# Experts stage of an encoder layer: the order of two products on the tensor engine, and three operations moved between engines

## The reference, cut to what matters

```
u = peer_u[idx]
a = gelu(einsum('td,ted->te', xb, u))
w = g * a
out = einsum('te,ted->td', w, peer_v[idx])
```

## Time and profile before

| | us |
|---|---|
| median of 3 runs | 4590.63 (4588.02 to 4590.66) |
| the profiled execution | 4585.41 |
| its span, first to last instruction | 4583.5 |
| PE busy in the span | 3587.8 (78%) |
| DVE busy | 3410.8 (74%) |
| ACT busy | 1299.2 (28%) |
| POOL busy | 943.7 (21%) |

### The profile page before, as it was taken

One profiled execution on the slowest core, in us unless ns is written; L12 is line 12 of the kernel. 1 busy time (PEld: TensorE's weight loads), 2 busy tenths in 40 slices (PEclk: granted clock), 3 DMA queues, 4 the chain that ended last, 5 costly groups with the idle time before them and its releaser, 6 DMA issues. The chain is left out here.

```text
span 4583.5 us, 62754 instructions
## 1 busy us (share of the span) xinstructions
PE 3587.8 (78%) x19538; PEld 1972.0 (43%) x19538; DVE 3410.8 (74%) x7568; ACT 1299.2 (28%) x2576; POOL 943.7 (21%) x1038
## 2 busy tenths in 40 slices
PE   7946567997899255333379999999999999999994
PEld 3525443553455122333334445444445445444442
DVE  1034341222679778999969999999999999999998
ACT  2132132211233223222223323323323323333321
POOL 0000000000000000000024444444444444444344
PEclk9966578998999677555589999999999999999997
DMA  2200012101110100333378888888888888888885
GB/s 87 82 3 0 0 80 101 42 14 60 65 38 31 58 0 15 97 111 111 99 271 329 337 320 324 337 328 329 328 330 330 335 318 331 338 326 335 323 323 192
DMA packets 238989, 856.89 MB, mean 187 GB/s; under 512 B 16080, under 2 KB 119312, under 8 KB 167440
## 3 DMA queue, kind: packets, MB, share of 16 engines
q0 software_dynamic: 73728, 536.90, 31.0%
q1 hardware_dynamic: 165136, 318.63, 20.0%
HBM read 792.55 MB, written 62.91 MB: 187 GB/s over the span
## 5 line engine op out<-in xcount | busy, mean ns | idle before, releaser
L1563 POOL COPY x_index<-expert 128x1 uint32 (+1 forms) x512 | 340.6, 665 | 3194.0 <-POOLq L1370 2316.4
L69 PE MATMUL x_ps_v<-x_v_hi,x_w_hi 128*128 128x512 f16 x1536 | 604.5, 394 | 137.2 <-DVE x_w_lo L1667 70.5
L1566 POOL DMA_INDIRECT x_rows<-in_peer_uv,x_index x512 | 579.6, 1132 | 406.9 <-POOL x_index L1563 393.1
L1637 DVE SCALAR_TENSOR_TENSOR acc<-x_rows,x_share,acc 128x1024 f32<-128x1024 f32 x512 | 655.0, 1279 | 0.0
L1721 PE MATMUL x_ps_a<-h_hi,x_u_hi 128*128 128x256 f16 (+1 forms) x2048 | 620.1, 327 | 15.4 <-ACT x_u_hi L1579 14.7
L1722 PE MATMUL x_ps_a<-h_lo,x_u_hi 128*128 128x256 f16 (+1 forms) x2048 | 619.8, 326 | 0.0
L70 PE MATMUL x_ps_v<-x_v_lo,x_w_hi 128*128 128x512 f16 x1536 | 603.7, 393 | 0.0
L71 PE MATMUL x_ps_v<-x_v_hi,x_w_lo 128*128 128x512 f16 x1536 | 602.8, 392 | 0.0
L1590 ACT ACTIVATE x_dots<-x_dots 128x1 f32<-128x1 f32 x512 | 103.9, 203 | 1335.1 <-DVE x_dots L1655 1335.1
L1446 PE MATMUL g_ps<-g_hot_g,g_hot_j 128*128 128x128 f16 x768 | 170.9, 310 | 325.7 <-DVE g_hot_g L1430 325.7
L1655 DVE CUSTOM_DVE_ANT_0 x_rows<-h_lo,x_rows 128x1024 f32<-128x1024 f32 x256 | 312.4, 1220 | 126.5 <-DMA x_rows<-in_peer_uv,x_index 125.3
(11 more groups left out here) (284 smaller groups left out, 6834.7 us busy)
## 6 DMA issues: line engine op xcount, KB each, us to landing
x_u_st<-in_peer_u_t SPq DMA_DIRECT2D x128, 512.0 KB, 6.1
x_v_st<-in_peer_v SPq DMA_DIRECT2D x128, 512.0 KB, 6.3
gate_scratch<-g_out SPq DMA_DIRECT2D x24, 2048.0 KB, 8.9
x_gate<-gate_scratch SPq DMA_DIRECT2D x32, 1024.0 KB, 8.7
x_gate<-gate_scratch SPq DMA_DIRECT2D x32, 512.0 KB, 3.8
m_w_st<-in_w_merge SPq DMA_DIRECT2D x8, 1536.0 KB, 6.4
k_w_st<-in_w_route SPq DMA_DIRECT2D x16, 576.0 KB, 3.7
x_rows<-in_peer_uv,x_index POOLq DMA_INDIRECT x512, 6.9
```

The source lines that it names most:

```text
L69: pe.matmul(out, lhs_hi, rhs_hi, start=first, stop=False)
L1563: pool.tensor_copy(index[:, m % RING:m % RING + 1], R.expert[:, tile, bass.ds(hk, 1)]).then_inc(index_ok, 1)
L1566: pool.indirect_dma_start(rows[:, m % RING], None, uv_all, bass.IndirectOffsetOnAxis(ap=index[:, m % RING:m % RING + 1], axis=0)).then_inc ...
L1637: dve.scalar_tensor_tensor(R.acc[:, DT + tile], rows[:, r, D:2 * D], share[:, s:s + 1], R.acc[:, DT + tile], ALU.mult, ALU.add).then_inc(v ...
```

## The change

It touches `experts` alone.

- **PE** works in the order: first product small of group i, second product large of group i - 1, first product large of group i, second product small of group i. The second product large of the last group stands behind the loop. The small first product now comes first and takes `k` = 0 to 3, so it is the one that waits for u.
- **DVE** follows: multiply and low part of the small block; the four additions of the previous group's large tiles; multiply, low part and `v_lo` of the large block; two additions of the small tiles. The 16 visits are spread anew by `AT`. DVE makes no `u_lo` any more.
- **Gates** are loaded into a staging buffer `gate_st`, and ACT copies them into `gate[P, E, ND]`, in which the values of one block of experts lie next to each other; one copy per block of tokens and group.
- **u_lo** is made on POOL from `u_st`, which ACT scales in place after it has made `u_hi` (`u_scaled`); four per group, behind the gathers of visits 12 to 15, for the next group.
- **Indices** are copied four at a time, for the four visits of a tile.
- The gelu result and its product with the gates share one buffer `w` of four slots in place of two buffers of two. The conversion of v on ACT stands in front of the gelu of the same step, where it stood behind.
- SP's loads are in a new order and wait with `wait_apart`.

```diff
-        RING = 4
+        RING, SLOTS_G = 4, 4
+        LARGE, SMALL = DENSE
+        TL, TS = LARGE[1] // P, SMALL[1] // P
-        gate = sb("x_gate", [P, ND, E], f32)
-        g_act, w = sb("x_g_act", [P, 2, 512], f32), sb("x_w", [P, 2, 512], f32)
+        gate_st = sb("x_gate_st", [P, LARGE[1], E], f32)
+        gate = sb("x_gate", [P, E, ND], f32)
+        w = sb("x_w", [P, SLOTS_G, 512], f32)
-        index = sb("x_index", [P, RING], u32)
+        index = sb("x_index", [P, 2, PER_TILE], u32)
+        AT = {("s", 0): 1, ("s", 1): 1, ("s", 2): 1, ("s", 3): 0,
+              ("l", 0): 2, ("l", 1): 1, ("l", 2): 2, ("l", 3): 1,
+              ("a", 0): 1, ("a", 1): 1, ("a", 2): 1, ("a", 3): 1,
+              ("v", 0): 2, ("v", 1): 1}
...
+            def group(i, first=False, last=False):
+                load_v(i, 0, first)
+                load_v(i, 1, first)
+                if not last:
+                    load_gates(i + 1, SMALL, 2 * i + 2)
+                    load_u(i + 1, 0)
+                    load_u(i + 1, 1)
+                    load_gates(i + 1, LARGE, 2 * i + 3)
+                load_v(i, 2, first)
+                if not last:
+                    load_u(i + 1, 2)
+                load_v(i, 3, first)
+                if not last:
+                    load_u(i + 1, 3)
...
+            def u_low(i, e):
+                pool.wait_ge(u_scaled, E * i + e + 1)
+                pool.tensor_tensor(u_lo[:, e].rearrange("p a b -> p (a b)"), u_st[:, e % 2],
+                                   u_hi[:, e].rearrange("p a b -> p (a b)"), ALU.subtract).then_inc(u_lo_ok, 1)
...
-                    pool.tensor_copy(index[:, m % RING:m % RING + 1],
-                                     R.expert[:, tile, bass.ds(hk, 1)]).then_inc(index_ok, 1)
-                    wait_apart(pool, index_ok, VISITS * i + m + 1)
+                    if m % PER_TILE == 0:
+                        pool.tensor_copy(index[:, tile % 2], R.expert[:, tile, bass.ds(hk, PER_TILE)]).then_inc(index_ok, 1)
+                        wait_apart(pool, index_ok, GT * i + tile + 1)
...
+                    if m >= VISITS - E and not last:
+                        u_low(i + 1, m - (VISITS - E))
+            for e in range(E):
+                u_low(0, e)
             group(0, True)
...
+                act.activation(u_st[:, e % 2], u_st[:, e % 2], ACT.Copy, scale=WSCALE).then_inc(u_scaled, 1)
+            def gates(n, part, taken):
+                t0, n_t = part
+                act.wait_ge(gate_in, 16 * n)
+                if taken is not None:
+                    act.wait_ge(w_ok, taken)
+                act.activation(gate[:, :, t0:t0 + n_t], gate_st[:, 0:n_t].rearrange("p t e -> p e t"),
+                               ACT.Copy).then_inc(gate_ok, 1)
...
+                gates(2 * i + 2, LARGE, None if first else A_STEPS * i)
+                for e in range(E):
+                    gelu(e, SMALL[1])
+                    if e:
+                        high(e - 1, SMALL)
+                    visits(("s", e))
+                high(E - 1, SMALL)
+                if not last:
+                    gates(2 * i + 3, SMALL, A_STEPS * i + E)
+                for t in range(TL):
+                    visits(("l", t))
+                for e in range(E):
+                    v_split(i, e, first)
+                    gelu(E + e, LARGE[1])
+                    if e:
+                        high(E + e - 1, LARGE)
+                    if not last:
+                        u_split(i + 1, e)
+                    visits(("a", e))
+                high(2 * E - 1, LARGE)
+                for t in range(TS):
                     visits(("v", t))
...
+                dve.wait_ge(gate_ok, 2 * i + 1)
+                for e in range(E):
+                    gated(e, SMALL)
+                    if e:
+                        low(e - 1, SMALL)
+                    visits(("s", e))
+                low(E - 1, SMALL)
+                for t in range(TL):
+                    if not first:
+                        add(V_STEPS * (i - 1) + TS + t, t % 2, t)
+                    visits(("l", t))
+                dve.wait_ge(gate_ok, 2 * i + 2)
+                for e in range(E):
+                    gated(E + e, LARGE)
+                    if e:
+                        low(E + e - 1, LARGE)
+                    visits(("a", e))
+                    dve.wait_ge(v_hi_ok, E * i + e + 1)
+                    dve.scalar_tensor_tensor(v_lo[:, e], v_st[:, e % 2], VSCALE, v_hi[:, e], ALU.mult,
+                                             ALU.subtract).then_inc(v_lo_ok, 1)
+                low(2 * E - 1, LARGE)
+                for t in range(TS):
+                    add(V_STEPS * i + t, t % 2, TL + t)
                     visits(("v", t))
...
+            def large(i):
+                pe.wait_ge(w_lo_ok, A_STEPS * (i + 1))
+                v_block(i, TS, LARGE, False)
+
             def group(i, first):
...
+                a_block(i, 0, SMALL, first)
+                if not first:
+                    large(i - 1)
+                a_block(i, E, LARGE, first)
+                pe.wait_ge(w_lo_ok, A_STEPS * i + E)
+                pe.wait_ge(v_lo_ok, E * (i + 1))
+                v_block(i, 0, SMALL, first)
             group(0, True)
             with pe.Fori(1, N_GROUPS) as i:
                 group(i, False)
+            large(N_GROUPS - 1)
```

More of the change, by code:

```diff
@@ L1496, in experts @@
         v_in = [sem("x_v_in0"), sem("x_v_in1")]
-        gate_in = [sem(f"x_gate_in{b}") for b in range(NBD)]
         rows_in = [sem(f"x_rows_in{r}") for r in range(RING)]
@@ L1620, in group, with gelu @@
-                high(n, k % 2, *before)
-                for t in range(DT):
-                    if t < E and not last:
-                        u_split(i + 1, t)
+                def gelu(k, n_t):
+                    act.wait_ge(a_mm, A_STEPS * i + k + 1)
+                    if not first or k >= SLOTS_G:
+                        act.wait_ge(w_lo_ok, A_STEPS * i + k - SLOTS_G + 1)
+                    act.activation(w[:, k % SLOTS_G, 0:n_t], ps_a[:, k % 4, 0:n_t], ACT.Gelu,
+                                   scale=1 / WSCALE).then_inc(gelu_ok, 1)
```

212 lines of the change are left out of this document (82 added, 130 removed).

## The result

The changed kernel takes **4948.89 us** (median, 4943.99 to 4962.31) against 4589.33, a ratio of 1.0789 (95% interval 1.0766 to 1.0813): 360 us slower. The prediction had the direction (chance 0.91), not the size: 4825, with 4890 as the upper end. The profiled execution takes 4943.99 us, its span is 4942.2.

What follows compares the result with a forecast made beforehand. DVE bounds the kernel at 68.55 us a group; after the change PE's 62.4 + tail 5.4 + holds 5.4 + clock 2.0 = 75.2, over 31 periods with start and end +235: 4825 us, range 4640 to 4890.

Steps and rivals of the forecast that it cites:

- PE's 62.4 us: PE's matmuls in one group of experts: 10 x 5.19 + 4 x 2.62 us, a floor in either order.
- DVE's terms: DVE's own work per group falls from 63.8 to 56.8 us: four u_lo removed (4.6), contiguous gate multiply saves 2.4.
- The tail: PE idle before the small second product, through gelu, multiply, low part, visit and v_lo: 5.4 us a group.
- The holds: POOL's u_lo stops DVE 2.3 us each; three before the fourth v_lo add 5.4 us of idle PE a group.
- The clock: After PE's idle stretch its matmuls run at the 1.2 GHz level: 2.0 us lost a group, bounds 0 and 2.3.
- The start: Group 0: first gather delayed to about 2338 us, nine visits, four steps; first second product begins near 2400 us.
- the end: End of the experts stage: 2400 + 31 x 75.2 + 34 = 4765 us against 4530.2, +235.
- Other parts, hidden: ACT's added scalings and gate copies (7 to 8 us a group), late v and u loads: no cost in the forecast.
- The chain of the v slots: Large block, v load (6.3 us) to the next v_lo: 12.7 us per two steps, under 14.0 with holds, costing nothing.
- Rival 4: POOL's holds also delay gathers and rows, so DVE starves too: period 79, 4940 us; chance 0.05.
- Indices by four only matter where DVE bounds: Three of four POOL index copies go (0.19 to 0.97 us each), rows come sooner; matters only where DVE bounds.
- the case without holds: Rival where POOL and DVE don't hold each other: period 69.8, 4655 us, up to 4700 with late v; chance 0.26.

Runs made afterwards that it cites:

- e9: Changed kernel with v_lo ahead of the multiply, u's low parts on DVE and the gate copies moved on ACT: 4654 us, ratio 1.0143.
- b3: Kernel before, in its old order, plus indices copied by four and contiguous gates: 4498 us, ratio 0.9812.
- e4: Changed kernel with POOL's u_lo cut to 32 of 1024 columns, other low parts of u left zero: 4898 us, one run.
- e1: Changed kernel with v_lo ahead of the multiply, low part and visit in DVE's large steps: 4813 us, ratio 1.0489.
- e5: Changed kernel with 64 extra matmuls, results overwritten, filling PE's idle time before the small second product: 4890 us, ratio 1.0658.
- e12: Changed kernel with gate copies moved, small second product's visits ahead of its adds, one more there, one less in the large: 4877 us, ratio 1.0637.
- b1: Kernel before plus only the indices copied by four: 4508 us, ratio 0.9819.
- e2: Changed kernel with u's low parts back on DVE, at the end of each large step: 4907 us, ratio 1.0694.

## Why the prediction was right in sign and wrong in size

- **PE's 62.4 us** stood. The new order's window of 78.17 us (3440.74 to 3518.91) has PE busy 64.80, which is 62.4 and the slow matmuls.
- **DVE's terms** stood. Not held, the multiply takes 683 to 691 ns (e9, b3), the forecast's 0.68. The Trainium skill ("VectorE: DVE Perf Modes", Mode 1× (REGULAR)) has the plain mode take strides too, at one result a cycle; 1090 ns with the strided gates against 691 ns without for the same multiply says otherwise, and the measurement decides.
- **The tail** of 5.4 us measured 5.5 in the block shown and in e4, and e1, which takes multiply, low part and visit (3.6 us) out of it, shortens it by 4.1.
- **The holds**: the Trainium skill ("GPSIMD Engine Reference", Specifications) names contention for DVE instructions with two SBUF inputs, and the runs agree: up to 2.34 us a hold. In the block shown the three add 1.86 + 2.34 + 0.74 = 4.9 us to DVE, where the forecast had 3 x 2.3. What they were worth was another thing: the forecast gave them 5.4 us a group of PE's idle time, e4 gives back 1.6. That 4825 is only 2.5% off is in part luck, for the 3.8 us too much here stand against more than 7 us too little in the hidden parts below.
- **The clock**: the small second product shown took 12.72 us (3506.19 to 3518.91) for the 2 x 5.19 = 10.38 of PE's pitch, 2.3 lost, 1.9 a group by e5; the forecast had 2.0.
- **The start** was right (first second product at 2394.89; forecast 2400), the end was not: last addition at 4887.48 + 1.22, 124 us behind the forecast's 4765. 31 x (79.5 - 75.2) = 133, less the 5 of the start, is within 4 us of that: it is the period. Of its 4.3 us, 3.6 are PE's gap (14.4 for 10.8) and 0.5 a wait of PE for DVE's additions (12.4 us over 13 times in 1900).
- **The step that failed is "Other parts, hidden"**, which set the new work on ACT, the late v and the u loads at nothing. The copies' own time was inside its bounds (3.92 + 2.06 us and four scalings of 1.04; "11 if ..."), and so was ACT's busy time (31.9 us a group for 30 to 33), but these parts were not hidden. The kernel without holds (e4) measures what they are worth: a period of 78.1 us, where the forecast's terms without holds give 69.8. Two things stand behind the 8.3 us.
  - *DVE's lateness.* The forecast let DVE begin the large steps as soon as PE delivered; the first gelu came 3.6 us late, in e4 too. With the gate copies moved and the visits made in DVE's idle time (e12) it comes 0.2 us late, the gap falls by 1.8 and the time by 72 us.
  - *The chain of the v slots.* It was put at 12.7 us, compared with PE's rate and with the 14.0 of two held steps, and so dropped. But nothing after the last two steps makes up for it. From the second `v_lo` (3491.42) to PE's start are 14.8 us in the block shown and 15.2 in the mean; in e4, with no hold, 15.6. Its load was the mis-sized part: 6.3 us is the median of all v loads before, the fourth v of a group takes 8.3 now and 8.9 in e4 (means of 24 groups). Why it takes so long was not tried; in e12 it takes 6.6.
  - *The two together.* The gap of e4 follows from them: the second `v_lo` ends 18.3 us after PE begins the block, where steps in time would have it at about 15.7 (2 x 5.19 and one step of 5.3), and 15.6 us of chain behind it end 13 us after PE's 20.9. In e12 12.6 us are left against 10.8: the last gelu is 4.7 us late, and a full hold in the tail makes that 7.9.
- **Rival 4** gave 4940 and a period of 79, by another mechanism: rows cost DVE 67.7 us in 1900, less than before. Its number is right by luck.
- **"Indices by four only matter where DVE bounds"** was right, and large where it does: 82 us.
- The range was too narrow above, since the late v was priced only in the case without holds, at no more than 2 us, and DVE's lateness nowhere.

## What to carry to other kernels

When an order puts one engine's whole chain behind another's last product, count the feeding engine's work phase by phase, not per period: here every phase ahead of the wait was nearly full, and a lateness of 3 us at the entry was never made up. Compare a chain of loads and slots with the end of the phase, and not only with the rate inside it. Put first, in each step, what the waiting engine needs (e1: 136 us for one moved operation), and let nothing stand in order behind a late load. Take a bundle of changes apart on the kernel before: two of these four parts alone make it 1.9% faster (b3, 4498 us), and that version beats both kernels. The four-value index copy alone (b1, 4508) can't be told from it.

## What had not been expected of the hardware

- ACT's copy with a read step of 16 bytes takes 3918 ns for 128x2048 and 2064 for 128x1024, a contiguous one of 128x1024 1043 ns: twice the time.
- An index copy of four values costs no more than one (571 ns in b1's mean, 665 in the kernel before, both with the waits for DVE in them), and each copy also put 0.77 to 0.8 us between itself and its gather (POOL's wait for `x_index`: 340.3 us over 440 times in the kernel before).
- Two limits that each seem to be worth little can be worth much together: e1 and e2 gave 136 and 42 us apart, 258 together, and on top of e12 311.
